# Two transformer blocks on one core: order of the passes of a product, and of the heads' work around two attentions

## The reference, cut to what matters

```
q = einsum(rms_norm(c_q, ..), w_uq)            # 8 heads x 96
k_nope, v_a = split(einsum(rms_norm(c_kv, ..), w_ukv))
k = concat(k_nope, k_r for each head)          # 8 x 96
q, k = rms_norm(q, mla_qn), rms_norm(k, mla_kn)
q, k = rope on the last 32 of the 96 columns
o_a = dense_causal_attention(q, k, v_a)
qd, kd = apply_rope(rms_norm(..)), 12 heads x 64 each, for the dilated attention that follows
```

## Time and profile before

| | |
|---|---|
| median of 3 runs | 1385.48 us (1384.81 to 1385.95) |
| profiled execution | 1386.78 us, its span 1385.0 us |
| TensorE, matmuls busy | 1313.3 us, 95%, 6436 instructions |
| TensorE, weight loads busy | 1079.2 us |
| VectorE busy | 921.2 us, 67% |
| ScalarE busy | 654.2 us, 47% |
| GpSimd busy | 110.8 us |
| mean granted clock of TensorE | 0.984 of full speed |
| read from memory | 268.27 MB, 194 GB/s over the span |

### The profile page before, as it was taken

One profiled execution on the slowest core, in us unless ns is written; L12 is line 12 of the kernel. 1 busy time (PEld: TensorE's weight loads), 2 busy tenths in 40 slices (PEclk: granted clock), 3 DMA queues, 4 the chain that ended last, 5 costly groups with the idle time before them and its releaser, 6 DMA issues.

```text
span 1385.0 us, 16064 instructions
## 1 busy us (share of the span) xinstructions
PE 1313.3 (95%) x6436; PEld 1079.2 (78%) x6467; DVE 921.2 (67%) x1233; ACT 654.2 (47%) x882; POOL 110.8 (8%) x145
## 2 busy tenths in 40 slices
PE   5999999998999999999898899999999969999998
PEld 5877888887887788887798876888877856788886
DVE  4866777766695777775766856766666785654444
ACT  4653544433463444443465454544446544554542
POOL 1001000000000100000223200000004310000000
PEclk9999999999999999999998999999999999999999
DMA  9615688873542568885253204876754420455550
GB/s 362 219 44 182 227 315 308 306 290 126 195 163 100 204 244 310 311 312 196 81 201 115 77 31 153 305 300 247 297 218 179 155 92 3 172 191 182 182 182 31
DMA packets 40362, 270.36 MB, mean 195 GB/s; under 512 B 4560, under 2 KB 4560, under 8 KB 12000
## 3 DMA queue, kind: packets, MB, share of 16 engines
q1 hardware_dynamic: 37712, 259.31, 50.6%
q0 software_dynamic: 2432, 8.98, 1.8%
q10 hardware_dynamic: 144, 1.05, 0.2%
HBM read 268.27 MB, written 1.05 MB: 194 GB/s over the span
## 4 chain that ended last, share of the span: by engine, by line
PE 82%; DVE 11%; ACT 3%; issue 2%; DMA 1%; POOL 1%; SPq 0%; DVEq 0%; ACTq 0%; POOLq 0%
PE ps L1445 24%; PE ps L1447 24%; PE ps L1446 24%; PE ps L1460 4%; DVE WB L1754 2%; PE ps L1545 2%; PE ps L1521 2%; PE ps L1430 1%; DMA RAW<-W 1%; ACT WB L1558 1%; DVE st L2030 1%; DVE st L1958 0%; DVE SCR L1860 0%; DVE XTL L1821 0%; PE ps L1527 0%
## 5 line engine op out<-in xcount | busy, mean ns | idle before, releaser
L1754 DVE TENSOR_TENSOR WB<-RAW,WB 128x2048 fp32r<-128x2048 f32 (+4 forms) x210 | 453.5, 2162 | 296.4 <-ACT WB L1558 296.0
L1445 PE MATMUL ps<-WB,XTH 128*128 128x512 f32 (+3 forms) x1176 | 458.5, 390 | 28.3 <-DVE XTL L1759 14.8
L1558 ACT ACTIVATE WB<-RAW 128x2048 fp32r<-128x2048 f32 (+4 forms) x210 | 379.7, 1810 | 218.9 <-PE ps L1447 207.4
L1447 PE MATMUL ps<-WB,XTL 128*128 128x512 f32 (+3 forms) x1176 | 449.5, 382 | 0.0
L1446 PE MATMUL ps<-WB,XTH 128*128 128x512 f32 (+3 forms) x1176 | 449.3, 382 | 0.0
L1445 PEld LDWEIGHTS ps<-WB,XTH 128*128 128x128 f32 x1176 | 224.8, 191 | 73.4 <-DVE XTL L1759 15.0
L1447 PEld LDWEIGHTS ps<-WB,XTL 128*128 128x128 f32 x1176 | 224.4, 191 | 38.8
L1446 PEld LDWEIGHTS ps<-WB,XTH 128*128 128x128 f32 x1176 | 224.7, 191 | 35.8
L1445 PE MATMUL ps<-WB,HTH 128*128 128x512 f32 (+1 forms) x452 | 178.8, 396 | 2.5 <-DVE HTL L1825 1.9
L1447 PE MATMUL ps<-WB,HTL 128*128 128x512 f32 (+1 forms) x452 | 178.4, 395 | 0.0
L1446 PE MATMUL ps<-WB,HTH 128*128 128x512 f32 (+1 forms) x452 | 178.3, 394 | 0.0
(11 more groups left out here) (173 smaller groups left out, 974.0 us busy)
## 6 DMA issues: line engine op xcount, KB each, us to landing
RAW<-W SPq DMA_DIRECT2D x220, 1024.0 KB, 4.9
RAW<-W SPq DMA_DIRECT2D x22, 768.0 KB, 4.3
VEC<-vecd POOLq DMA_DIRECT2D x10, 512.0 KB, 7.8
RAW<-W SPq DMA_DIRECT2D x8, 512.0 KB, 3.4
RAW<-W SPq DMA_DIRECT2D x4, 648.0 KB, 5.7
RAW<-W SPq DMA_DIRECT2D x4, 576.0 KB, 3.9
GB<-xTd ACTq DMA_DIRECT2D x1, 1024.0 KB, 7.6
X<-xd SPq DMA_DIRECT2D x1, 1024.0 KB, 17.7
```

Source lines behind the costliest of these rows:

```text
L1445: eng.matmul(ps, xh, hi[:, j, c0:c0 + cw], start=first and j == 0, stop=False)
L1447: op = eng.matmul(ps, xl, hi[:, j, c0:c0 + cw], start=False, stop=last and j == n - 1)
L1558: return eng.activation(dst, src, f, **k)
L1754: eng.tensor_tensor(WB[:, it["raw"], 0:w], RAW[:, it["raw"], 0:w], WB[:, it["high"], 0:w].bitcast(F32), ALU.subtract).then_inc(*up("wl", n))
```

## The change

Three edits. First, a "mm" makes the three passes one after the other over all its k-tiles (and PSUM banks). It waits for the high halves only ("th", "wh"), makes high by high, then the two other passes, each behind its own wait: for the first item of a product (`fresh`, in `partial` for every item) the low weight goes before the low x, for the others the low x goes before the low weight. Second, in `attention` the low halves that are open at a unit's start are put behind the unit's transposes, difference and filling pieces. Third, the heads' norms and rotations stand earlier, and the filling pieces are spread in another way over the units.

```
@@ linear, linear2, partial: "mm" gets one more argument
-  ..., pad[t] if it is its[0] else 0)
+  ..., pad[t] if it is its[0] else 0, it is its[0])          # linear
+  ..., pad[t] if it is ia[0] and c == 0 else 0, it is ia[0])  # linear2
+  ..., 0, True)                                               # partial
@@ attention, in the loop over units
-                lows()
+                old = list(low)
                 if 1 <= k <= n:
                     turns(units[k - 1], pads[k - 1] if k <= len(pads) else 2)
...
                 if 1 <= k <= n and units[k - 1]["joint"]:
                     ends(units[k - 1])
+                lows(old)
                 if k >= 2:
                     values(units[k - 2])
@@ even layer, second block
                     run(linear("mla_w_uq_2", 0, ltw, put_H("mq", c, 2304 + c * 384, 2688 + c * 384, qw)))
+                mch, mr = {}, {}
+                e_box = [{"free": list(e_free[0])}, {"free": list(e_free[1])}]
+                def heads(n, x_, ww, nm):
+                    for t in range(2):
+                        mr[n, t] = []
+                        mch[n, t] = qk_pair(("mla", n, t), x_[:, t, :], 8, 96, 16, 64, COS[:, t, 8:40:2],
+                                            SIN[:, t, 8:40:2], sm[nm], ww[t], E[:, n, :], e_box[n], mr[n, t])
+                heads(0, MQ, qw, "mla_q_norm_2")
+                mch[0, 0][0]()
...
                 run(linear("mla_w_ukv_2", 3, ltw, put))      # k
+                heads(1, MK, kw, "mla_k_norm_2")
+                mch[1, 0][0]()
+                mch[0, 0][1]()
...
                 run(linear("mla_w_ukv_2", 3, ltw, put))      # v
+                mch[0, 1][0]()
+                mch[1, 0][1]()
...
-                run(weave(dils(0, 1), [[mch[0, 0][0], mch[1, 0][0]], [gs[0], mch[0, 0][1], mch[0, 1][0]],
-                                          [gs[1], mch[1, 0][1], mch[1, 1][0]], [gs[2], mch[0, 1][1]],
-                                          [gs[3], mch[1, 1][1]]]))
+                run(weave(dils(0, 1), [[gs[0], mch[1, 1][0], mch[0, 1][1]], [gs[1], mch[1, 1][1]],
+                                       [gs[2], ch[0, 0][0], ch[0, 1][0]], [gs[3]]]))
...
+                ch[0, 0][1]()
+                ch[1, 0][0]()
                 fill = lined(dils(2, 3, 5), [
-                    None, [ch[0, 0][0], ch[0, 1][0]], None,
-                    [ch[0, 0][1], ch[1, 0][0]], None,
-                    [ch[0, 1][1], ch[1, 1][0]], None,
-                    [ch[1, 0][1], ch[2, 0][0]], [ch[1, 1][1], ch[2, 1][0]],
-                    [ch[2, 0][1], ch[3, 0][0]], [ch[2, 1][1], ch[3, 1][0]],
-                    [ch[3, 0][1]], None, [ch[3, 1][1]]])
+                    None, [ch[0, 1][1], ch[1, 1][0]], None, [ch[1, 0][1], ch[2, 0][0]],
+                    [ch[1, 1][1], ch[2, 1][0]], None, [ch[2, 0][1]],
+                    None, [ch[2, 1][1], ch[3, 0][0]],
+                    [ch[3, 0][1], ch[3, 1][0]], None,
+                    [ch[3, 1][1]], None])
...
-                attention(units, 96 ** -0.5, fill, (3, 2, 2, 2, 2, 2, 1, 0))
+                attention(units, 96 ** -0.5, fill, (4, 3, 2, 2, 2, 0, 0, 0))
@@ odd layer, second block
-                           [gs[2], ch[1, 1][0], ch[1, 0][1]], [gs[3], ch[1, 1][1]]]))
+                           [gs[2], ch[1, 1][0], ch[1, 0][1]], [gs[3], ch[1, 1][1]], [ch[3, 0][0], ch[3, 1][0]]]))
...
+                ch[3, 0][1]()
+                ch[4, 0][0]()
                 fill = lined(part((2, 5)), [
-                    None, [ch[3, 0][0], ch[3, 1][0]], None,
-                    [ch[3, 0][1], ch[4, 0][0]],
-                    None, [ch[3, 1][1], ch[4, 1][0]],
-                    None, [ch[4, 0][1]],
-                    [ch[4, 1][1]], [lambda: turn_qk(3, 0, 8, twm), lambda: turn_qk(3, 1, 8, twm)],
+                    None, [ch[3, 1][1], ch[4, 1][0]], None,
+                    [ch[4, 0][1]], None,
+                    [ch[4, 1][1]], None,
+                    [lambda: turn_qk(3, 0, 8, twm), lambda: turn_qk(3, 1, 8, twm)],
                     [lambda: turn_qk(4, 0, 12, twm), lambda: turn_qk(4, 1, 12, twm)]])
...
-                attention(units, 0.125, fill, (3, 1, 2, 2, 2, 1), pads=(2, 2, 3, 3))
+                attention(units, 0.125, fill, (3, 2, 2, 1, 1, 0), pads=(2, 2, 3, 3))
@@ TensorE's program
-            def mm(it, t, lhs, outs, first, last, after, fr, pad):
+            def mm(it, t, lhs, outs, first, last, after, fr, pad, fresh):
                 for e in fr:
                     on.wait_ge(*at(*e))
                 busy(outs[0][0], pad)
-                for e in after:
-                    on.wait_ge(*at(*e))
-                on.wait_ge(*at("wl", it["id"]))
+                for kind, key in after:
+                    on.wait_ge(*at({"tl": "th", "pl": "ph", "xl0": "xh0"}[kind], key))
+                on.wait_ge(*at("wh", it["id"]))
...
+                x2 = [stationary(lhs, it["a"] + j, t) for j in range(n)]
+                for b, c0, cw, _ in outs:
+                    for j in range(n):
+                        eng.matmul(banks[b][:, 0:cw], x2[j][0], hi[:, j, c0:c0 + cw], start=first and j == 0, stop=False)
+                for low_w in ((True, False) if fresh else (False, True)):
+                    if low_w:
+                        on.wait_ge(*at("wl", it["id"]))
+                    else:
+                        for kind, key in after:
+                            on.wait_ge(*at(kind, key))
+                    end = low_w != fresh
+                    for o, (b, c0, cw, key) in enumerate(outs):
+                        for j in range(n):
+                            op = eng.matmul(banks[b][:, 0:cw], x2[j][0 if low_w else 1], (lo if low_w else hi)[:, j, c0:c0 + cw],
+                                            start=False, stop=last and end and j == n - 1)
+                        keys = ([key] if key else []) + ([it["id"]] if t and o == len(outs) - 1 else [])
+                        if keys and end:
+                            op.then_inc(*up("mm", *keys))
```

More of the change, by code:

```diff
@@ L374, in slot @@
                 do("mm", it, t, lhs, [(b, 0, w, (g, t) if it is its[-1] else None)], it is its[0], it is its[-1],
-                   wanted(after[t], lhs, it), fr if it is its[0] else [], pad[t] if it is its[0] else 0)
+                   wanted(after[t], lhs, it), fr if it is its[0] else [], pad[t] if it is its[0] else 0, it is its[0])
                 if t:
@@ L423, in slot @@
                    it is its[-1], wanted(after[t], lhs, it), fr if it is its[0] else [],
-                   pad[t] if it is ia[0] and c == 0 else 0)
+                   pad[t] if it is ia[0] and c == 0 else 0, it is ia[0])
             for t in range(2):
@@ L465, in one @@
                 do("mm", it, t, lhs, [(ps[t][c][0], c * 512, 512, (g, t, c) if end else None) for c in range(2)],
-                   first and n == 0, end, wanted(after, lhs, it), ps[t][0][1] + ps[t][1][1] if first and n == 0 else [], 0)
+                   first and n == 0, end, wanted(after, lhs, it), ps[t][0][1] + ps[t][1][1] if first and n == 0 else [], 0, True)
                 if t:
@@ L1435, in mm @@
                 busy(outs[0][0], pad)
-                for e in after:
-                    on.wait_ge(*at(*e))
-                on.wait_ge(*at("wl", it["id"]))
+                for kind, key in after:
+                    on.wait_ge(*at({"tl": "th", "pl": "ph", "xl0": "xh0"}[kind], key))
+                on.wait_ge(*at("wh", it["id"]))
                 w, n = it["w"], it["n"]
                 hi, lo = (WB[:, p, 0:n * w].rearrange("p (k w) -> p k w", k=n) for p in (it["high"], it["raw"]))
-                for o, (b, c0, cw, key) in enumerate(outs):
+                x2 = [stationary(lhs, it["a"] + j, t) for j in range(n)]
+                for b, c0, cw, _ in outs:
                     for j in range(n):
-                        xh, xl = stationary(lhs, it["a"] + j, t)
-                        ps = banks[b][:, 0:cw]
-                        eng.matmul(ps, xh, hi[:, j, c0:c0 + cw], start=first and j == 0, stop=False)
-                        eng.matmul(ps, xh, lo[:, j, c0:c0 + cw], start=False, stop=False)
-                        op = eng.matmul(ps, xl, hi[:, j, c0:c0 + cw], start=False, stop=last and j == n - 1)
-                    keys = ([key] if key else []) + ([it["id"]] if t and o == len(outs) - 1 else [])
-                    if keys:
-                        op.then_inc(*up("mm", *keys))
+                        eng.matmul(banks[b][:, 0:cw], x2[j][0], hi[:, j, c0:c0 + cw], start=first and j == 0, stop=False)
[13 more added lines that the diff above has]
+                            op.then_inc(*up("mm", *keys))
             def turn(g, srcs, dst, rows, b, by, after, fr, pad):
```

7 lines of the change are left out of this document (removed).

## The result

The changed kernel takes 1361.08 us (median of 4 runs, 1359.15 to 1365.26), the kernel before beside it 1385.56 us (4 runs, 1384.81 to 1385.95): ratio 0.9828, 95% interval 0.9802 to 0.9854. The forecast was 1360.0. The profiled execution took 1359.15 us with a span of 1357.3.

A forecast was written before the change was run, and what follows sets the result against it. TensorE's queue was taken as the bound, busy 1313.3 of 1385.0 us. Gains 15.5 + 7.5 + 3 = 26 us off 1386.8 give 1360.8; less 1.3 for the median, 1359.5, rounded to 1360; range 1350 to 1374.

The forecast's parts named there:

- Products: Matrix products: high by high pass starts before low halves are ready, shortening TensorE's waits; 15.5 us (7.5 + 2.1 + 5.9).
- the two w_ple_gate: First block's two layers: the 2.60 us wait for the low weight shrinks to 0.6; gain 3.4 us in each layer.
- the opening: Second block's start: waits of 1.20 us for a low weight and 1.06 for a low x shrink; 2.1 us.
- The start: Kernel's start: earlier first products gain 0 because VectorE's copy sets the next transposes; ends -1.7 and +1 us.
- The price of waits inside the products: Two more semaphore waits for each of 210 weight pieces: taken as nothing, upper end 0.08 x 420 = 34 us.
- The rival built on the Trainium skill's reorder window: All 210 product pieces: waits inside break overlap of weight loads and matmuls, 34 us against 26, 1393 us; chance 0.04.
- Heads and even attention: Second block's even layer: earlier norms and rotations, respread fillers; 0.8 us before scores, 7.5 in all, ends 3 and 11.5.
- Odd attention: Second block's odd layer: rotations ahead of the last difference, 3 us gain despite a new 5 to 6 us wait.
- rival (e): Even layer: queue is emptied of low halves at product start anyway, so moving them behind changes under 1 us; no separate chance.
- part 4: Odd layer's attention: all four rotations precede the last difference, VectorE waits out exponentials; 3 us, ends 0 and 8.5.
- One sign named as speaking against the forecast: Whole kernel: total idle time of TensorE not falling below 50 us would show the forecast wrong.
- The other signs: Waits: none over 0.7 us before products but at 728, none before 96-row transposes, no 4 us in even attention.

The follow-up runs named there:

- Experiment 3: Products' new order of passes alone, with every wait back in front of the item, against the kernel before: 1387.32 us, ratio 1.0011.
- the products' kernel: The kernel before with only the new order of the products (`mm` and its calls): 1367.97 us, ratio 0.9876.
- experiment 10: The changed kernel with low halves back in front in attention and last items' three passes fully bank by bank: 1349.27 us, ratio 0.9736.
- experiment 11: Experiment 10 with the odd layer's filler spread over the units and the last rotation behind the last difference: 1346.43 us, ratio 0.9714.
- experiment 2: The changed kernel with `mm` as before, so all other hunks without the products' new order: 1377.19 us, ratio 0.9939.

## Why the prediction was right, and where it was not

**Products.** Forecast 15.5, measured 17.6 alone. By its trace: 3.3 and 3.5 us in the two w_ple_gate (forecast 3.4 each), 0.7 ahead of the first and 1.5 between them, 2.6 us from the second layer's end to the even layer's first scores (2.1 forecast for the opening and 0.4 at 706), 5.9 us from there to the odd layer's first scores (forecast 3.85). The mechanism held in every stage looked at. One gave something back: at the second layer's opening a wait of 1.0 us for low x went (341.61 before), but the transposes of X behind it wait 2.4 us for VectorE where they waited 1.2, and the clock in the 3 us behind them is 0.72 where it was 1.00. The start was costed at nothing (-1.7 to +1); the first scores of the kernel come 0.5 us earlier in after (69.87, 70.36 before).

**The price of waits inside the products.** Taken as nothing, with 34 us as upper end. Experiment 3 and the passes shown there give no price that can be measured. The upper end itself was too high: its 420 waits are, counted in the program, 316 (688 at the products in place of 372), so 25 us at 0.08. The rival built on the Trainium skill's reorder window ("TensorE: Matmul & The Clock Gate", "Architectural detail") is gone: a wait already satisfied does not break the overlap of weight loads and matmuls in these traces.

**Heads and even attention.** Forecast 7.5 (0.8 ahead of the scores, the rest in the attention). The table gives 2.0 us ahead of the scores (86.7 from the second layer's end to them in the products' kernel, 84.7 after) and 7.35 in the attention, 9.35 in all; undone, 10.4. The mechanism was right and the size low: the clock stood only at the upper end of the range, and it was real: 0.78 to 0.94 and 0.83 to 1.00.

**Odd attention.** Forecast 3, with a new wait of 5 to 6 us. The wait is 6.86, the stage gives 5.0 (52.8 to 47.8 us between the table's fifth and sixth rows), and undone the plan costs 5.0. What follows the wait, put down at 6 us up to the next scores, took 5.6 (1111.64 to 1117.19). The size that was off is VectorE's sum ahead of it: the last difference was forecast 40.3 us behind the stage's first scores (1095.7 to 1136), and its transposes start 38.3 us behind them (1073.32 to 1111.64).

**What failed: the low halves behind the pieces.** The prediction dealt with this edit in rival (e) as worth under 1 us in the even layer. In part 4 it saw that VectorE would wait out the exponentials (1.5 to 2 us a unit) and never asked what filling that time was worth. It costs 8.8 us. The step that was missing is the one that the working asked for elsewhere: name what is queued behind the moved instruction. A low half of 2.28 us was put into the one round in which a normalise of 0.9 us follows, for which TensorE waits with nothing left to do. No part of the prediction looked at any of the four places: two are in the first block, which runs through the same `attention`, and two at the ends of the second block's second attentions. I had read the edit as one of the second block's first attentions. The waits grew by 1.0 to 1.8 us at each end (0.37 to 1.44, 0.38 to 1.44, 0.30 to 1.27, 0.68 to 2.48: 4.9 us), and 3.3 us of the 6.86 are of the same edit.

**The tail.** Also missed: two banks in one item are completed pass by pass, so the first is ready 2 matmuls before the end instead of 6, and VectorE's last evacuations start later: 16.1 to 16.9 us from the last opening to the end.

**The sum.** Forecast 26 us off the profiled execution; 27.6 came (1386.8 to 1359.15), 24.5 by medians. By the pieces it is 17.6 + 10.4 + 5.0 less the 8.8 that the low halves cost, 24.2. So the right total came from three gains that were under-counted by 7.0 us (26 against 33) and a loss of 8.8 that was not counted. The mechanisms of the three gains were right; that the total came out within 1.1 us of the forecast is luck, since errors of 7.0 and 8.8 us went opposite ways. One sign named as speaking against the forecast did appear: TensorE's idle time, 56.1 us, did not fall below 50. The normalise waits and the last difference are 13.5 us of it, 7.3 more than before, and following them up is what led to the faster versions. The other signs came out on the forecast's side: from 120 us on the only wait over 0.71 us ahead of a product is the 1.52 at 720.91, no 96-row transpose waits, the even attention has no wait of 4 us, and the second block's longest is ahead of the last unit's transposes in the odd layer.

**What stays open.** Why the same wait is followed by a stretch at 1.2 GHz in one execution and not in the next was not tried. Nor were the 2.2 us that experiment 10 has over its tail. That experiment 11 gained over experiment 10 rests on its stage, 3.8 us shorter in one profile of each with the wait of 3.5 us for the last difference gone, more than on the two medians.

## What to carry to other kernels

Put the wait for a late operand directly ahead of the first instruction that needs it, and order the work so that what needs only early operands comes first: here the places of the waits were worth 17.6 us and the order by itself nothing. A long instruction with a far deadline belongs where its engine already waits, not where a short one follows that another engine stands still for; when a shared routine's order is changed, look at all its callers. And when a sum comes out right, still look for lines that have grown in the list of waits: two of them here, 7.3 us more than before, belong to an edit whose undoing gave 8.8 us.

## What the runs showed of the hardware

The granted clock goes with a part of the spread between executions of one kernel: the slowest of after (1365.26 us) had a mean of 0.988, the other three 0.991, which is 4 us of work; yet one of those three took 1362.72 and another 1359.15. Waits of TensorE of one length are followed by 3 to 6 us at 1.2 GHz in one execution and by none in another: behind the wait of 2.48 us the mean clock of the next 3 us was 0.50 in the kernel of experiment 2 and 1.00 in after. In the thirteen profiles none of the 28 normalise waits of 0.30 to 0.68 us has a lower clock behind it, and 6 of the 24 of 1.27 to 2.48 us have one. A longer wait thus costs more than its length, but not each time. The row of after:

```profile
1146.00:1149.00 3.00, 3.00 (x15) 2.47 (x14) 1.02 (x2) 0.20 (x2) 0.00 (x0) 1.00 0.00 0
```

The clock of a window is a mean, so 3 us at 0.50 are 1.5 us of work lost. The profiles with fewer long waits have the higher mean clock: 0.984 before, 0.991 after, 0.994 and 0.995 in experiments 10 and 11. A single run can mislead: after ranged over 6.1 us, the kernel before over 1.1 in the same set.
